# A hybrid decoder layer: two token tiles instead of four projected ahead, kept on chip, their attentions staggered between key folds, and later loads issued at other places

## The reference, cut to what matters

```python
def _layer(x, p, past_k, past_v, ...):
    proj = _rmsnorm(x, norm_attn_g) @ w_in            # q, k, v, u: 4 x 512 columns
    k_all, v_all = past with the new k, v
    attn = softmax(q1 k1) v - lam * softmax(q2 k2) v  # 4 heads, causal, relative bias
    pool_out = windowed means of u (2, 4, 8, 16), minus u, @ pool_w
    x = x + concat(attn, pool_out) @ w_out
    x = x + _peer(_rmsnorm(x))                        # the expert layer
    x = x + sigmoid(_rmsnorm(x) @ w_pl_gate) * (p @ w_pl)
    return final rmsnorm(x), k, v, last rows of u

def _peer_block(xb, wq, sub_keys, u_tab, v_tab):      # 8 heads, 128 + 128 keys
    q = xb @ wq; s = q . sub_keys                     # top 16 of each half, then top 16 pairs
    idx, gate = top-16 experts of 16384, softmax
    h = gelu(xb . u_tab[idx])
    return sum(gate * h * v_tab[idx])
```

## Time and profile before

| | us |
|---|---|
| median of 3 runs | 3407.74 (3406.8 to 3418.14) |
| the profiled execution | 3413.72 |
| its span, first to last instruction | 3411.9 |
| its mean granted PE clock | 0.846 |

### The profile page before, as it was taken

One profiled execution on the slowest core, in us unless ns is written; L12 is line 12 of the kernel. 1 busy time (PEld: TensorE's weight loads), 2 busy tenths in 40 slices (PEclk: granted clock), 3 DMA queues, 4 the chain that ended last, 5 costly groups with the idle time before them and its releaser, 6 DMA issues.

```text
span 3411.9 us, 53263 instructions
## 1 busy us (share of the span) xinstructions
...
## 2 busy tenths in 40 slices
...
GB/s 305 141 84 74 383 421 417 422 371 404 316 332 417 388 389 419 385 401 362 416 412 409 378 406 416 418 420 412 420 419 415 408 420 420 408 417 420 419 417 200
DMA packets 213299, 1270.91 MB, mean 372 GB/s; under 512 B 26640, under 2 KB 29992, under 8 KB 72240
## 3 DMA queue, kind: packets, MB, share of 16 engines
...
HBM read 1238.68 MB, written 28.92 MB: 372 GB/s over the span
## 4 chain that ended last, share of the span: by engine, by line
DMA 28%; PE 13%; DVE 7%; POOL 3%; issue 2%; ACT 2%; DVEq 1%; SPq 0%; another core or an unknown queue 0%; POOLq 0%; ACTq 0%
DMA ring<-in_uv,idx 27%; PE sc L870 6%; DVE ring L1649 4%; PE sc L903 3%; POOL ring L1818 2%; DMA front<-in_c_band_sp 1%; PE route L844 1%; POOL front L1834 1%; ACT diag L1216 1%; PE sc L872 1%; DVEq L1659 1%; PE work L891 1%; ACT hgelu L1211 0%; PE sc L587 0%; PE sc L863 0%
## 5 line engine op out<-in xcount | busy, mean ns | idle before, releaser
L1818 POOL DMA_INDIRECT ring<-in_uv,idx x1056 | 1228.1, 1163 | 1843.2 <-PE sc L872 1402.2
L870 PE MATMUL sc<-ring,diag 32*32 32x512 f32 x8192 | 1254.0, 733 | 691.9 <-ACT diag L1216 669.5
L1649 DVE CUSTOM_DVE_ANT_0 ring<-ring,xn_cur 128x1024 f32<-128x1024 f32 x1056 | 1278.6, 1222 | 648.9 <-DMA ring<-in_uv,idx 644.6
L872 PE MATMUL sc<-ring,diag 32*32 32x512 f32 x8192 | 1253.5, 733 | 0.0
L870 PEld LDWEIGHTS sc<-ring,diag 32*32 32x32 f32 x8192 | 274.2, 118 | 1485.8 <-ACT diag L1216 1126.6
L1211 ACT ACTIVATE hgelu<-hdot 128x2 f32<-128x2 f32 x528 | 107.4, 203 | 1855.2 <-DVE hdot L1649 1852.6
L1216 ACT ACTIVATE diag<-gate_d,hgelu 128x32 f32<-128x32 f32 x1056 | 281.7, 314 | 21.2
L872 PEld LDWEIGHTS sc<-ring,diag 32*32 32x32 f32 x8192 | 272.9, 118 | 0.0
L463 PE MATMUL sc<-big,front 128*128 128x512 f32 x512 | 238.5, 616 | 4.8 <-DVE front L1309 4.8
L1211 ACT ACT_TABLE_LOAD x124 | 159.1, 1283 | 2.2
L844 PE MATMUL route<-big,xnT 128*128 128x256 f32 x576 | 143.6, 405 | 0.0
...
## 6 DMA issues: line engine op xcount, KB each, us to landing
...
ring<-in_uv,idx POOLq DMA_INDIRECT x1056
...
```

The costliest lines, as they stand in the source:

```text
L870: pe.matmul(sc[own, 0, :], diag[own, r, :], uv_rows[own, r, D:D + W4], start=opens_sum, stop=closes).then_inc(row_added[r], 1)
L872: pe.matmul(sc[other, 1, :], diag[own, r, :], uv_rows[own, r, D + W4:2 * D], start=opens_sum, stop=closes).then_inc(row_added[r], 1)
L1649: dve.tensor_tensor_reduce(uv_rows[:, k % RING, 0:D], uv_rows[:, k % RING, 0:D], xn_cur[:, :], 1.0, 0.0, ALU.mult, ALU.add, hdot[:, n % 2, ...
L1818: pool.indirect_dma_start(uv_rows[:, k % RING, :], None, uv, bass.IndirectOffsetOnAxis(ap=idx[:, n % PH, j:j + 1], axis=0)).then_inc(row_i ...
```

## The change

Tiles 0 and 1 alone are projected in the lead-in. ACT writes their q, k, u and v straight to the buffers from which attention reads them, which are now apart for the two tiles; the outputs that are results are stored from there, and nothing is loaded back. The two attentions stand three slots apart; tile 1's band and pool products use the route bank. The fold no longer stands ahead of all slots but takes two of its 16 products in each of slots -15 to -8, with sub-keys and `wq_t` in `gate_d`, `xn_cur`, `xnT` and a piece of the ring, in the two sum banks. Tiles 2 to 7 are projected in slots 0 to 59, one in 10 slots. The twelve constants are issued by ACT, and POOL waits for the second piece of `w_in` before it loads. POOL's first fetch no longer waits for x1; fetch 4 waits for stores of k, u, v, and fetch 7 for x1.

Later on: attention 2 to 7 start at slots 67, 84, 101, 123, 145 and 167. Their q, k, u loads are issued one slot after head 2 of the attention before has been transposed, the bands one slot after head 3. In slot 62 SP issues the loads of attention 2 before v and `w_out`. One more route is streamed (29). The page loads stand later against the slots in which PE reads them (6 for 2, 5 for 1), values take 4 slots a batch instead of 2, tile 3 is deferred too, and gate jobs have slots of their own.

```diff
-STREAMED = 28
-
-
-
-LEAD = 20
+STREAMED = 29
...
+LEAD = 19
...
 def turn_x_slot(t):
-    return 14 * (t - 4) if t >= 4 else -LEAD + max(0, 4 * t - 2)
+    return 10 * (t - EARLY) if t >= EARLY else -LEAD + t
 
 
 def project_slot(t, o, half):
-    return 14 * (t - 4) + (2, 3, 5, 6, 8, 9, 11, 12)[2 * o + half] if t >= 4 else -LEAD + 4 * t + o
+    return 10 * (t - EARLY) + 2 + 2 * o + half if t >= EARLY else -LEAD + 2 * t + o // 2
 
 
 def kept_slot(t, o):
     s = project_slot(t, o, 1)
-    return s + 1 if t >= 4 else s
-
-
-SAMPLE_NORM, SAMPLE_TURN, SAMPLE_PROJECT, SAMPLE_KEEP = 50, 56, 58, 61
-W_IN_FREE = 60
-OLD_KEYS = 62
-
-Attention = namedtuple("Attention", "load turn band pool chunks scores keys weights norm heads out")
+    return s + 1 if t >= EARLY else s
...
+def fold_slot(hp):
+    return -LEAD + 4 + hp // 2
+
+
+ROUTE_0 = -4
+SAMPLE_NORM, SAMPLE_TURN, SAMPLE_PROJECT, SAMPLE_KEEP = 52, 58, 60, 63
+W_IN_FREE = 62
+OLD_KEYS = 65
...
 def attention_slots(t):
 
     if t < EARLY:
-        b = -LEAD + 4 + 6 * t
-        scores = [[b + 2 + h] for h in range(H)]
-        return Attention(b - 1, b, b + 1, b + 2, [(0, (t + 1) * T)], scores, [b + 3 + h for h in range(H)],
-                         [b + 3 + h for h in range(H)], (b + 6, b + 6), b + 7, (b + 8, b + 8))
-    b = {2: 64, 3: 80, 4: 96, 5: 118, 6: 140, 7: 162}[t]
+        b = -LEAD + 2 + 3 * t
+        first = b + 2 + t
+        scores = [[first + h] for h in range(H)]
+        weights = [first + 2 + h for h in range(H)]
+        end = weights[-1]
+        return Attention(None, None, b, b + 1, b + 2, [(0, (t + 1) * T)], scores, weights, weights,
+                         (end + 1, end + 1), end + 2, (end + 3, end + 3 + (t == 0)))
+    b = {2: 67, 3: 84, 4: 101, 5: 123, 6: 145, 7: 167}[t]
...
+    if t == EARLY:
+        load = load_s1 = W_IN_FREE
+    else:
+        load, load_s1 = (ATT[t - 1].weights[h] + 1 for h in (H - 2, H - 1))
+    return Attention(load, load_s1, b, b + 1, b + 2, chunks, scores, keys, weights, (end + 1, end + 2), end + 3,
...
-C_PAGE = C0 + 12
+C_PAGE = C0 + 18
 C_SCORES = C_PAGE + NPAGE + 2
 C_VALUES = C_SCORES + 11
-C_OUT = C_VALUES + 2 * DB
-C_END = C_OUT + 9
-
-
-GATE_JOBS = [(3, 36), (4, 40), (0, 43), (5, 48), (1, 51), (6, 56), (2, 59), (7, 64), (8, NN)]
-DEFERRED = (0, 1, 2)
+C_OUT = C_VALUES + 4 * DB
+C_END = C_OUT + 17
+
+
+DEFERRED = (0, 1, 2, 3)
+GATE_JOBS = [(4, 322), (0, 342), (3, 361), (5, 384), (1, 404), (6, 448), (2, 468), (7, 512), (8, NN * PAIRS)]
...
+        keys_sb = [gate_d[:, :, :, :].rearrange("p a b c -> p (a b c)").rearrange("p (a b) -> p a b", b=NK),
+                   xn_cur[:, :].rearrange("p (a b) -> p a b", b=NK)]
+        wq_st = [xnT[:, :, :].rearrange("p a b -> p (a b)"), cut(ring_a, 14848, D)]
+        stage = [cut(fr, i * 2048, KD, 256) for i in range(2)]
...
+                q, k, u, v = ([cut((fr, a)[i], 8192 + o * W4, W4) for i in range(2)] for o in range(4))
+                bc = [cut(a, 10240, W4), cut(a, 11264, W4)]
+                pw, bp, dT = (cut(a, at, W4) for at in (10752, 11776, 12288))
+                S = [cut(a, 12800 + i * 512, 2, 256) for i in range(2)]
+                xT = [cut(a, 13824, KD, T), cut(a, 8192, KD, T)][t]
+                xr = [[xn_next[:, 0:W4], xn_next[:, W4:D]], [cut(a, 14848, W4), cut(a, 15360, W4)]][t]
+                avs = [xn_next[:, W4:D], cut(a, 15360, W4)][t]
+                qT = [cut(a, 15872, H, T), cut(fr, 10752, H, T)][t]
                 kT = x2[:, :].rearrange("p (h n) -> p h n", h=H)
-                v = [cut(a, 15872, W4), cut(fr, 10752, W4)]
                 wo = cut(a, 0, KD, D)
                 at_ = [xT[:, c, :] for c in range(4)]
...
-
-        B = [attention_bufs(0)] * EARLY + [attention_bufs(EARLY)] * (NT - EARLY)
+                return Bufs(q[t], k[t], u[t], u[0], bc[t], bp, dT, pw, S, xT, at_, avs, xr, qT, kT, v, wo)
...
+        def band_bank(t):
+            return RT if t == 1 else WK
...
             for s in range(-LEAD, 0):
                 front_step(s)
-                if s == -7:
+                for hp in range(2 * PH):
+                    if s == fold_slot(hp):
+                        fold_keys(hp)
+                if s == ROUTE_0 - 1:
                     turn_xn(0)
-                if s >= -6 and s < -3:
-                    route(s + 6)
+                if ROUTE_0 <= s < ROUTE_0 + 3:
+                    route(s - ROUTE_0)
...
+            for dst, src in (
...
+                act.dma_start(dst, src).then_inc(const_in, 16)
...
+                if t == EARLY and o == 0:
+                    act.wait_ge(ready[S1], filled(S1, ("out", EARLY - 1, 1)))
+                if t >= EARLY and stored(o, t - 1):
+                    act.wait_ge(qkuv_out[o], 16 * stored(o, t - 1))
                 act.wait_ge(ready[b], filled(b, ("project", t, o)))
-                act.activation(kept[o], bank[b], ACT.Copy, scale=st[:, XR + t % 2:XR + t % 2 + 1]).then_inc(free[b], 1)
+                to = (B[t].q, B[t].k, B[t].u, B[t].v[t])[o] if t < EARLY else kept[o]
+                act.activation(to, bank[b], ACT.Copy, scale=st[:, XR + t % 2:XR + t % 2 + 1]).then_inc(free[b], 1)
...
+            pool.wait_ge(w_in_in[1], 16)
+            for i in range(2):
+                pool.dma_start(keys_sb[i], keys_t[i * PH:(i + 1) * PH].rearrange("h d k -> d h k")).then_inc(keys_in, 16)
             for hp in range(2 * PH):
                 if hp >= 2:
-                    pool.wait_ge(ready[S1], filled(S1, ("fold", hp - 2)))
+                    pool.wait_ge(ready[A1], filled(A1, ("fold", hp - 2)))
                 pool.dma_start(wq_st[hp % 2], wq_t[hp * T:(hp + 1) * T, :]).then_inc(wq_in[hp % 2], 16)
...
                 if k == 0:
                     pool.wait_ge(ready[S1], filled(S1, ("out", EARLY - 1, 1)))
+                if k == 4:
+                    for o in range(1, 4):
+                        pool.wait_ge(qkuv_out[o], 16 * stored(o, EARLY - 1))
+                if k == RING - 1:
                     pool.wait_ge(x1_out, 16 * 2 * EARLY)
                 if k >= RING:
...
-                    return page_at(i - PAGES) + 2
-                return value_at((i - NPAGE - PAGES) // NPG) + 1
+                    return page_at(i - PAGES) + 6
+                return value_at((i - NPAGE - PAGES) // NPG) + 5
...
+                src = (B[t].q, B[t].k, B[t].u, B[t].v[t])[o] if t < EARLY else kept[o]
+                sp.dma_start((q_d, nk_p, u_d, nv_p)[o][tile_rows(t), :], src).then_inc(qkuv_out[o], 16)
...
+            def load_early():
+
+                sp.dma_start(B[0].bc, c_bands[tile_rows(0), :]).then_inc(early_in, 16)
+                sp.dma_start(B[1].bc, c_bands[tile_rows(1), :]).then_inc(early_in, 16)
+                sp.dma_start(by_group(B[0].pw), pool_w).then_inc(early_in, 16)
+                sp.dma_start(by_group(B[1].bp), c_band_prev).then_inc(early_in, 16)
 
             def load_attention(t):
 
                 a = B[t]
                 for o in range(3):
-                    sp.wait_ge(qkuv_out[o], 16 * (t + 1))
-                if t == 0:
-                    for b in (S0, S1):
-                        sp.wait_ge(ready[b], filled(b, ("fold", 2 * PH - 1)))
-                elif t == 1:
-                    sp.wait_ge(ready[WK], filled(WK, ("pool", 0)))
-                elif t == EARLY:
-                    sp.wait_ge(ready[TB], filled(TB, ("old k", 1)))
+                    sp.wait_ge(qkuv_out[o], 16 * stored(o, t))
+                if t == EARLY:
+                    sp.wait_ge(ready[S0], filled(S0, ("project", NT)))
                 else:
-                    sp.wait_ge(o_sq, t)
-                by_group = lambda ap: ap.rearrange("p (g t) -> p g t", g=H)
+                    for b in (TA, TB)[:1 if t <= 4 else 2]:
+                        sp.wait_ge(ready[b], filled(b, ("weights", t - 1, H - 2)))
                 sp.dma_start(a.q, q_d[tile_rows(t), :]).then_inc(att_in, 16)
                 sp.dma_start(a.k, nk_p[tile_rows(t), :]).then_inc(att_in, 16)
                 sp.dma_start(a.u, u_d[tile_rows(t), :]).then_inc(att_in, 16)
-                sp.dma_start(a.bc, c_bands[tile_rows(t), :]).then_inc(att_in, 16)
-                sp.dma_start(by_group(a.pw), pool_w).then_inc(att_in, 16)
-                if t:
-                    sp.dma_start(a.up, u_d[tile_rows(t - 1), :]).then_inc(att_in, 16)
-                    sp.dma_start(by_group(a.bp), c_band_prev).then_inc(att_in, 16)
+                sp.dma_start(a.up, u_d[tile_rows(t - 1), :]).then_inc(att_in, 16)
+
+            def load_bands(t):
+
+                a = B[t]
+                if t > EARLY:
+                    for b in (TA, TB)[:1 if t <= 4 else 2]:
+                        sp.wait_ge(ready[b], filled(b, ("weights", t - 1, H - 1)))
+                sp.dma_start(a.bc, c_bands[tile_rows(t), :]).then_inc(band_in, 16)
+                sp.dma_start(by_group(a.bp), c_band_prev).then_inc(band_in, 16)
+                sp.dma_start(by_group(a.pw), pool_w).then_inc(band_in, 16)
 
```

(13 more changed lines are left out.)

274 lines of the change are left out of this document (153 added, 121 removed).

## The result

The changed kernel took **3251.36 us** (median of 4 runs, 3248.36 to 3252.52) against 3408.35 us before (4 runs, 3406.8 to 3418.14): ratio **0.9532**, 95% interval 0.9513 to 0.9551. The prediction was 3230, range 3175 to 3290. The profiled execution took 3252.52 us with a span of 3250.5, so 161 us less than that of before; the prediction's sum had 178.

What follows compares the result with a forecast made beforehand. DMA engines at 420 GB/s bound the kernel, beside the lead-in and lost DMA time. Terms -133 + 9 - 41 - 18 + 5 = -178 took 3413.72 to 3236; allowing 6 us for the profiled run, 3230 us, range 3175 to 3290.

Steps and rivals of the forecast that it cites:

- part A: Lead-in up to the first gather: shortened from 347.8 to 212 us, less 3 us lost; -133 us, bounds -112 and -150.
- part D: The samples: page-load wait goes (-10), values' loads spread over four slots (-7), output's `w_out` (-1); -18 us, 0 to -25.
- Part B: Slots 0 to 63: two more tiles projected there, extra bytes and PE falling slightly behind; +9 us, bounds +7 and +37.
- Part C: Attention 2 to 7: stalls at attention 3 to 7 go (-30, -6), attention 2's moves (-5); -41 us, bounds 0 and -60.
- The rival of a PE-bound stretch: Slots 0 to 59: PE becomes the bound, 6.2 us a slot instead of 5.8, +28 us, about 3258; chance 0.15.
- The stand of DVE: Slot 70, attention 2: DVE stands some 30 us in `pooled(2)` awaiting samples' stores; loss 6 us instead of 11.
- The 6 MiB beside the gathers: Attention 2: v and `w_out`, queued ahead of the samples' stores, load at 79 to 90 GB/s, not through before 100 us.
- Part E: One more streamed piece and one more tile stored and loaded, 1 MiB each: +5 us; gate-job waits add 0, at most +10.
- Later stalls that only change their releaser: Rival on attention 2 to 7: DVE's wait costs what PE's did, attention 3 and 4 still lose 20 us each; 3271, chance 0.12.
- A fold that does not cover the chain: Rival on the lead-in: fold slots do not cover the attention's chain, +32 us at most, 3262; chance 0.08.
- The other three: Rivals: PE-bound slots 0 to 59 (0.15); half clock (0.02); chain to first gather hardly shortens, 3350 to 3400 (0.03).
- Half clock through slots 0 to 62: Rival: PE at half clock there, about 10.8 us a slot, +310 us, 3540, slower than before; chance 0.02.

Runs made afterwards that it cites:

- the run with the stores first: Changed kernel with the loads of v and the output weights issued in slot 63 behind the samples' stores instead of slot 62 ahead of them: 3238.2 us.
- the kernel with late and joined waits: Changed kernel, attention 3 to 7 loads two slots before use, PE's q/k turn also awaiting bands, SP's loads awaiting the previous attention's norm: 3292.76 us.
- the kernel with all three edits: Changed kernel with samples' loads ahead of tile 2's store, samples' stores ahead of v and output weights, ACT's copy ahead of exponents: 3224.72 us.

## Why the prediction was right, point by point

The time lies inside the range, and each of the named mechanisms was seen. The sum was 17 us too large: 10 are missing in part A and 10 in part D, and B and C came some 5 better than forecast.

- **Part A, -133, came as -122.6** (dots of slot 8). The start was as worked out: the first fold product at 89.18 us, forecast 89. The step that was mis-sized is the fold's slots: 71 us were forecast for the fold's eight pairs, and they took 83 (89.18 to 172.0), 10 to 13.5 us a pair from the third on. The forecast counted engine time, 2 to 4 us a slot of attention under 9.4; it left out that ACT's copy stood behind the exponents of a later head. The run with the copy first gives the mis-sized term back: -11.7 at the first gather, 4.4 of it by shorter products. The forecast's 71 held two errors: the fold alone takes 64 us (the fold in one block), and the chain beside it was not wholly covered. What follows the fold took 46.5 us instead of 52 (of which 5 were the author's estimate for PE at half clock; the granted clock was 0.89 from 172 to 219 us), which hid half of the miss. The first dot came at 232.8, forecast 228, and 3.6 us more than forecast were lost from the first gather to slot 8.
- **Part B, +9, came as +6.8**, at 5.77 us a slot with PE at 94%. That the bytes alone count, and PE's nearness nothing, is shown by the run with less projection. The rival of a PE-bound stretch falls.
- **Part C, -41, came as -43.5** (slots 64 to 184), but with other shares: 29.8 up to slot 104 (forecast 35) and 13.7 behind it (forecast 6). Attention 2 gained nothing (14 us lost, as against 11 before; forecast 6). The stand of DVE was forecast to within a microsecond, 30.39 us, and so was it that the DMA engines have bytes meanwhile; its price was not. The step left out is the restart: with no gather issued for 33 us, the engines fell to 247 GB/s from 670 to 700 us, 12 us lost, and the run with the stores first got 13.2 us back. Attention 3 to 7 gained more than the 36 of the sum: 41 by the kernel with late and joined waits. Read by its dots (slot 104 at 895.6 us, slot 184 at 1370.9) it is 26.5 up to slot 104 (forecast 30) and 15.4 behind it (forecast 6). The two errors nearly cancel, so that C's total came out is in part luck.
- **The 6 MiB beside the gathers** were forecast at 79 to 90 GB/s. The 79 is that of the earlier trace rows; the 90 was the author's estimate, and no row shows it. The landing times of v and of the two halves of `w_out` in the changed kernel:

```profile
DMA to landing us min/median/max: 53.1/53.1/53.1
```

```profile
DMA to landing us min/median/max: 51.8/60.5/69.2
```

  Nine pieces and v, 4.25 MiB, were issued from 591.53 us on, and v, issued at 595.7, landed at 648.8: 78 GB/s beside the gathers. The 4 MiB of `w_out` were through at 672, 23 us later, 179 GB/s. No gather was issued after 645.62, and all queues together moved 392 to 410 GB/s in each 5 us from 650 to 670: the "rest at full rate" of the prediction.
- **Part D, -18, is the term that failed.** Slots 184 to 320 gained 6.5 us and moved 0.7 MB more (2 us), so D came as about -8. The page load's wait went, as forecast, but it is worth 5 us rather than 10. The stretch of the values did lose less, as forecast: slots 208 to 320, before and after,

```profile
1658.00:2298.00 640.00, 463.61 (x4340) 172.38 (x4332) 434.43 (x1065) 160.64 (x450) 304.96 (x275) 0.82 1.00 409
```

```profile
1492.00:2132.00 640.00, 450.57 (x4368) 173.57 (x4360) 428.26 (x1049) 155.78 (x447) 321.11 (x283) 0.82 1.01 414
```

  lost 17 us and 9. The spacing is not the cause, since with the old spacing nothing was lost; the loads' new distance of five slots was not put back, and the cause stays open. Against both stands the one wait that was not foreseen, the samples' loads behind tile 2's store in slot 194: 21.26 us instead of 8.6. Of `C0` the sum had only looked at what follows it, not at what SP does in the same slot. Of the 6.9 us that slots 184 to 208 gained, some 6 are 2.5 MB that moved behind slot 208.
- **Part E, +5.** Slot 320 to the end cost 4.4 us; with the 0.7 MB ahead of it that is some 6, if all of it is E's, which no run separates.
- **The rivals.** Later stalls that only change their releaser: true of attention 2 alone. A fold that does not cover the chain: true for nearly half, since of the 41 us that lay under the fold 19 came back as a longer fold. The other three did not come. Half clock through slots 0 to 62 was far off: 0.98 was granted from 277 to 600 us. As for an `out` twice as long, in the kernel before single matmuls of it took up to 1222 ns where the median is 593, but the slowest half of one in attention 2 to 7 took 9.48 us (at 1351.28) and the fastest 7.03.

Left open: which of the two waits in the last step of part C weighs more, what of the samples' stall remains when `wqk`'s blocks do not stand ahead (13 us of wait are left in the kernel with all three edits), and why slots 208 to 320 lost less.
